# Page turns ahead of the latent queries, and the query weights on ScalarE's queue, in the sample stage of a two-layer decoder step

## The reference, cut to what matters

```python
past_ckv = cache_ckv[l, page_table].reshape(n_db, past_len, KV_LORA)
past_kpe = cache_kpe[l, page_table].reshape(n_db, past_len, QK_ROPE)
q_lat = jnp.einsum('bthn,chn->bthc', q_nope, w_uk)
s_past = (jnp.einsum('bthc,bsc->bhts', q_lat, past_ckv)
          + jnp.einsum('bthr,bsr->bhts', q_rope, past_kpe)).astype(jnp.float32) * MLA_SCALE
...
o_lat = (jnp.einsum('bhts,bsc->bthc', p[..., :past_len], past_ckv) + ...)
return jnp.einsum('bthc,chv->bthv', o_lat, w_uv)
```

## Time and profile before

| | |
|---|---|
| median of 3 runs | 1995.31 us (1993.66 to 1998.4) |
| the profiled execution, its time | 1996.14 us |
| its span in the profile | 1994.5 us, 29478 instructions |
| TensorE matmul busy | 1699.0 us, 85% of the span |
| VectorE, ScalarE, GpSimd busy | 37%, 28%, 39% |
| mean granted clock of TensorE | 0.926 |
| the sample stage | about 988.8 us to 1131 us of the span |

### The profile page before, as it was taken

The page is one execution under the profiler, slowest core; times in us unless marked ns, Lnnn a source line. Parts: engine busy times, 40 slices in busy tenths (PEclk is TensorE's granted clock), DMA queues, the critical chain, the costliest instruction groups (busy, mean ns, idle before and its releaser), DMA issues. The chain is left out here.

```text
span 1994.5 us, 29478 instructions
## 1 busy us (share of the span) xinstructions
PE 1699.0 (85%) x11101; PEld 1600.1 (80%) x11101; DVE 734.3 (37%) x1413; ACT 568.2 (28%) x1252; POOL 786.6 (39%) x905
## 2 busy tenths in 40 slices
PE   2899998899999999999597499974599996887893
PEld 2899997799999999999574399973499996766892
DVE  4015200576576566576323000016223001884004
ACT  4112101344444444444222000014122102773003
POOL 3433332255455455554450133312333231673420
PEclk9999999999999999999779699995799997997895
DMA  3112222111121121111297511113333133231105
GB/s 129 43 53 74 95 94 75 39 62 59 51 67 56 59 67 57 59 52 56 82 358 257 212 54 53 42 53 117 124 130 110 44 126 123 85 97 29 65 19 180
DMA packets 95255, 179.72 MB, mean 90 GB/s; under 512 B 11714, under 2 KB 60891, under 8 KB 94723
## 3 DMA queue, kind: packets, MB, share of 16 engines
q1 hardware_dynamic: 73892, 115.68, 17.7%
q0 software_dynamic: 10368, 31.47, 4.4%
q10 hardware_dynamic: 10880, 31.04, 4.3%
HBM read 130.34 MB, written 49.89 MB: 90 GB/s over the span
## 5 line engine op out<-in xcount | busy, mean ns | idle before, releaser
L602 POOL TENSOR_SCALAR b_prob<-b_prob,b_share 128x896 f32<-128x896 f32 (+7 forms) x128 | 97.3, 761 | 201.6 <-DVE b_share L802 199.8
L110 PE MATMUL ps<-a_xh,w_hi_a 128*128 128x344 f32 x552 | 118.5, 323 | 5.4 <-POOL w_lo_a L95 5.4
L110 PE MATMUL ps<-a_xl,w_hi_a 128*128 128x344 f32 x552 | 117.6, 321 | 0.0
L110 PE MATMUL ps<-a_xh,w_lo_a 128*128 128x344 f32 x552 | 116.9, 320 | 0.0
L702 ACT ACTIVATE b_pth<-ps 128x512 fp32r<-128x512 f32 (+1 forms) x160 | 86.2, 554 | 104.1 <-PE ps L927 94.4
L693 ACT ACTIVATE b_prob<-ps,b_least 128x896 f32<-128x896 f32 (+7 forms) x128 | 94.9, 743 | 58.6 <-DVE b_least L793 57.6
L793 DVE TENSOR_REDUCE b_least<-ps 128x1 f32<-128x896 f32 (+7 forms) x128 | 96.2, 751 | 37.0 <-PE ps L913 36.3
L110 PE MATMUL ps<-xh,w_hi_f 128*128 128x344 f32 x432 | 93.2, 325 | 19.0 <-POOL w_lo_f L95 19.0
L807 DVE TENSOR_TENSOR b_ptl<-ps,b_pth 128x512 fp32r<-128x512 f32 (+1 forms) x160 | 99.0, 632 | 27.0 <-ACT b_pth L702 26.0
L92 POOL TENSOR_TENSOR w_hi_a<-w_raw_a,ones 128x1024 fp32r<-128x1024 f32 x23 | 44.9, 1951 | 160.1 <-PE ps L110 160.1
L110 PE MATMUL ps<-xo_h,w_hi_d 128*128 128x344 f32 x384 | 82.5, 323 | 24.8 <-POOL w_lo_d L95 24.8
(11 more groups left out here) (252 smaller groups left out, 4801.0 us busy)
## 6 DMA issues: line engine op xcount, KB each, us to landing
w_raw_a<-in_w_tiles SPq DMA_DIRECT2D x23, 512.0 KB, 3.5
c_pages<-in_cache_pages SPq DMA_DIRECT2D x64, 160.0 KB, 7.8
c_pages<-in_cache_pages POOLq DMA_DIRECT2D x64, 160.0 KB, 5.6
w_raw_f<-in_w_tiles SPq DMA_DIRECT2D x20, 512.0 KB, 4.9
gate_scratch<-a_stage ACTq DMA_DIRECT2D x16, 512.0 KB, 2.6
b_gate<-gate_scratch SPq DMA_DIRECT2D x64, 128.0 KB, 2.6
oh_scratch<-b_oh POOLq DMA_DIRECT2D x64, 128.0 KB, 2.1
ol_scratch<-b_ol POOLq DMA_DIRECT2D x64, 128.0 KB, 2.1
```

The source lines that it names most:

```text
L110: mm = nc.tensor.matmul(ps[:, bank + c, 0:CH], wt, xt[:, k0 + k, c * CH:(c + 1) * CH], start=first and x == 0, stop=last and x == 2)
L602: nc.gpsimd.tensor_scalar(prob[:, n % 4, 0:keys], prob[:, n % 4, 0:keys], share[:, n % 4:n % 4 + 1], 1.0, ALU.mult, ALU.mult).then_inc(nor ...
```

## The change

The two loads of `c_wk` are issued by ScalarE at the start of its program in place of SyncE, which goes on to the pages straight from the page table. TensorE turns the four items of chunk (0, 0) first; the wait for `c_wk` and the latent queries stand behind them, ahead of turn (0, 1, 0). ScalarE copies its two items of that chunk, (0, 0, 0) and (0, 0, 2), before it waits for the latent queries. The diff in full:

```diff
--- before.py
+++ after.py
@@ -1038,8 +1038,6 @@
         @block.sync
         def _(sp):
             nc.sync.dma_start(table[:], a["page_table"].rearrange("(o b) n -> o (b n)", o=1)).then_inc(table_in, 16)
-            for i in range(2):
-                nc.sync.dma_start(wk[i][:], a["w_uk_turned"][i * H // 2:(i + 1) * H // 2].rearrange("h p k -> p h k")).then_inc(wk_in, 16)
             sp.wait_ge(table_in, 16)
             for r in range(ROUNDS):
                 for c in range(CHUNKS):
@@ -1085,6 +1083,13 @@
 
         @block.scalar
         def _(act):
+            for i in range(2):
+                nc.scalar.dma_start(wk[i][:], a["w_uk_turned"][i * H // 2:(i + 1) * H // 2].rearrange("h p k -> p h k")).then_inc(wk_in, 16)
+            def keep(r, c, s):
+                to, src = keep_turned(act, r, c, s)
+                nc.scalar.activation(to, src, ACT.Copy).then_inc(act_kept, 1)
+
+            keep(0, 0, 0), keep(0, 0, 2)
             act.wait_ge(cleared, 1)
             act.wait_ge(q_made, 1)
             for c in range(2):
@@ -1094,10 +1099,6 @@
                 nc.scalar.activation(q_b[e * ROPE:(e + 1) * ROPE, 2 + e, :, 0:H], g.qs_rope[:, 0:H, :].rearrange("p h b -> p b h"),
                                      ACT.Copy).then_inc(q_kept, 1)
 
-            def keep(r, c, s):
-                to, src = keep_turned(act, r, c, s)
-                nc.scalar.activation(to, src, ACT.Copy).then_inc(act_kept, 1)
-
             def exponents(r):
                 act.wait_ge(maxed, r + 1)
                 nc.scalar.activation(prob[:, 0:PAST + 1], prob[:, 0:PAST + 1], ACT.Exp, bias=stat[:, 0:1],
@@ -1110,7 +1111,7 @@
                 nc.scalar.activation(pt[:, 4 * i:4 * i + 4, :], ps[:, 6 - i % 2, :].rearrange("p (k n) -> p k n", k=4),
                                      ACT.Copy).then_inc(p_act, 1)
 
-            for c in range(CHUNKS):
+            for c in range(1, CHUNKS):
                 keep(0, c, 0), keep(0, c, 2)
             keep(1, 0, 0)
             exponents(0)
@@ -1194,13 +1195,6 @@
 
         @block.tensor
         def _(pe):
-            pe.wait_ge(wk_in, 32)
-            for h in range(H):
-                for c in range(2):
-                    mm = nc.tensor.matmul(ps[:, 6, c * P + h * DEC:c * P + (h + 1) * DEC],
-                                          wk[h // 8][:, h % 8, c * P:(c + 1) * P], g.qs_nope[:, h, :], start=True, stop=True)
-            mm.then_inc(q_made, 1)
-
             def kept(n):
 
                 pe.wait_ge(act_kept if n % 2 == 0 else dve_kept, n // 2 + 1)
@@ -1270,6 +1264,12 @@
 
             for s in range(QUAD):
                 turn(0, 0, s)
+            pe.wait_ge(wk_in, 32)
+            for h in range(H):
+                for c in range(2):
+                    mm = nc.tensor.matmul(ps[:, 6, c * P + h * DEC:c * P + (h + 1) * DEC],
+                                          wk[h // 8][:, h % 8, c * P:(c + 1) * P], g.qs_nope[:, h, :], start=True, stop=True)
+            mm.then_inc(q_made, 1)
             for c in range(1, CHUNKS):
                 turn(0, c, 0), turn(0, c, 1)
                 score(0, c - 1)
```

## The result

The changed kernel takes 2000.62 us (median of 14 runs, 1997.6 to 2003.91), the kernel before 1997.13 us in the 14 runs that now stand beside it (1990.66 to 1999.99). The ratio is 1.0025, with a 95% interval of 1.0017 to 1.0033. Of 1997 us that is **+5.0 us** (3.4 to 6.6): a small loss, clear of the scatter. The ratio is worked out from all these runs and is not the quotient of the two medians, which lie 3.5 us apart; that too is within the interval.

The account below looks back on a forecast made before the run. One TensorE chain was taken to bound the stage. From page landing 1006.3, turns 6.2, latent queries 10.5, turns 3.4 and scores ended at 1029.95 against 1023.44: +6.5 us, forecast 2001.8, range 1997.0 to 2005.0.

Parts of the forecast that it names:

- the sum: End of chunk 0's scores: 1029.95 against 1023.44, +6.5 us, with everything behind keeping its pace and shifting.
- What bounds the stage, and that a shift goes through whole: From the first latent query, one TensorE chain with copies; a microsecond at 1023 is a microsecond at the end.
- The order costs, the queue does not: Stage start: new order puts TensorE's first work behind the later transfer; moving wk's issue gains zero, at most 1.0 us.
- T0: Landing of SyncE's eighth page, which the first turn awaits: 1006.3, bounds 1001.3 to 1008.3.
- The pick among the bounds: Eighth page's issue to landing: 9.2 us taken, from the same page in the second round; bounds 4.2 and 11.2.
- the two sums: The forecast sum, and the one by the DMA rule alone: T0 stays 1008.3, sum 2.0 us larger.
- Four turns: TensorE's first turns after T0: three at 1.70 us and one at 1.1, 6.2 us, to 1012.5.
- Latent queries: 64 matmuls after the four turns: 28 at 0.108 and 36 at 0.2075, 10.5 us, to 1023.0.
- Turns and scores behind: After latent queries: two turns at 1.70, 3.4 us; chunk 0's scores 2.7 us plus 0.85 lost, ending at 1029.95.
- the clock that holds: Rival: high clock lasts through the latent queries, scores end 1024.3, +0.9 us, 1996.2; chance 0.14.
- the early pages: Rival: without wk in SyncE's queue pages land by 1003.0 to 1001.3, +3.2 to +1.5 us, 1998.5 to 1996.8; chance 0.16.

Follow-up runs that it names:

- the run with wk late: Changed kernel, with ScalarE issuing wk (query weights) only after SyncE's first eight pages have landed; 2023.23 us, one run.
- 120 idle transposes: Changed kernel plus 120 identity transposes into an unused bank ahead of TensorE's first turn, results unused; 2002.9 us, one run.
- the run with 148 transposes: Changed kernel plus 148 identity transposes into an unused bank ahead of TensorE's first turn, results unused; 2001.88 us, one run.
- the last run: Kernel before, with a semaphore per wk half, new_rep's small loads behind all pages, 32 idle transposes ahead of latent queries; 1990.92 us against 1995.28, ratio 0.9973.

## Why the prediction was right

It forecast a loss, at 2001.8 us with a range of 1997.0 to 2005.0; measured were 2000.62, or 5.0 us by the ratio where the sum gave 6.5. That the two absolute times lie only 1.2 us apart is in part luck: the kernel before now has a median of 1997.13, where the prediction started from 1995.31. By its steps:

- *What bounds the stage, and that a shift goes through whole.* Shown. The shift is 5.8 us at the end of the scores and 6.0 at the last mix, both counted from the table. Later transfers took up none of it.
- *The order costs, the queue does not.* Shown by the two halves: 1.0036 for the order alone, 1.0011 for the queue alone. They needn't add up, since in the new order wk is no longer waited for; the queue alone costs its 1.4 us by the later landing of wk, which the old order waits for.
- *T0, first turn.* Predicted 1006.3, measured 1007.34, of which 0.24 is the later start of the stage. The pick among the bounds (9.2 us of flight) was 0.9 too low; it was 10.1. One sentence of the working was wrong: that the pages "run beside wk" once wk is in another queue. They stood until 1.70 of wk's 2.1 MB had moved, as the 0.00 MB above show. The rule cited from the Trainium skill ("DMA: Bandwidth & Descriptors", "Issuing engines are not separate DMA queues") put the value of the move at nothing, and the two kernels with the new order and equal first turns, 18.31 and 18.39, agree with it. The 2.0 us that separated the two sums rested on one late landing (11.2 us in the earlier trace rows; 9.8 to 11.2 over six profiles with that queue), of which some 0.7 may be the queue's.
- *Four turns.* Predicted 6.2 us, measured 5.6: the clock rose 2.9 us after the first turn and not 5.1. The rule of the Trainium skill that transposes don't bring the full clock ("TensorE: Matmul & The Clock Gate", Part 4 (PE-mode transpose)) doesn't hold for the transposes of this kernel, which the profile lists as MATMUL: TensorE had been idle for 25 us, ran only turns, and the clock rose. The moment is not to be relied on: in the run with wk late, where TensorE had also waited, it rose only 6.0 us after the first turn, and the four turns took 6.6 us.
- *Latent queries.* Predicted 28 at the high clock and 36 at the low, 10.5 us; measured 4.1 us at the high clock, then 0.50, 9.7 us in all. The mechanism stood, the size was 0.8 off. About 40 of the 64 ran at the high clock. The prediction's remark that above 42 the shift would be under 4 us doesn't follow from its own prices: at 0.0995 us saved for each, 42 give 5.1 us, and it takes about 53.
- *Turns and scores behind.* Predicted 3.4 + 3.55 us, measured 3.6 + 3.2 (1022.70 to 1026.29 to 1029.49).

So the terms were off by +1.0, -0.6, -0.8 and -0.2. The path and the waits were right; that the sum, 6.5 where the profile has 5.8 to 6.2, is closer than some of its terms is luck, since a later landing and a faster TensorE partly cancel. The ratio's 5.0 has both within its interval (3.4 to 6.6). Of the rivals, the clock that holds is refuted by the run with 148 transposes, and the early pages by the landing itself: only without wk's bytes ahead do they come early.

Not shown is why the clock holds for different times under the latent queries: 4.1 us in the changed kernel, 4.1 with the order alone, 4.0 with 120 idle transposes, 2.6 with 148, and 5.0 in the last run, with 0.56 us of waiting in it. Nor is it shown why it comes back after 2.7 to 3.1 us of turns in four of the profiles and after 4.6 to 6.0 in six. Each of these is one profile.

## What to carry to other kernels

When two transfers feed one engine, give it first the work of the transfer that lands first, and count landings from a trace rather than the order of issues: here wk was whole at 998 and the pages ten microseconds later, and the order made the loss. Moving a load to another engine's queue did not let the other transfers pass it, and the load itself landed no sooner. A wait for two halves of a load can be split, but look at the next transfers in line before counting the gain: here it was gone, by a wait of 2.5 us and the slow clock behind it, until a row of small loads was moved out of their way.

## What the runs showed of the hardware

- A load of 2.1 MB that is issued 3 us ahead holds the pages of another hardware queue back almost completely: 1.70 MB against 0.00 in 991 to 996 us of the changed kernel. The same load, issued behind page traffic, gets a fifth of the bytes moved (0.78 of 3.60 MB), and its second half needs 27 us in place of 9.9.
- Matmuls with 8 columns lost the 2.4 GHz clock each time they met it: after 1.4 us in the output product, 2.6 to 4.1 us in the latent queries of four runs, even after 14 us at 1.00, though TensorE is busy without a gap, and after 5.0 us in the last run.
- Idle transposes of the identity, at no cost of time since TensorE was waiting, brought the clock up ahead of real work: the last run's first 32 latent queries ran at 1.00. With 3.2 us of idling behind 120 of them the clock was gone.
